# Two-block transformer kernel: in the second layer the gates of the recurrence's branch come first, with their sigmoid, and that branch's products are dealt out in the rounds of heads and softmax

## The reference, cut to what matters

```python
(k_raw, v_raw, i_raw, ff_raw, fb_raw, q_raw, qh_raw, gh_raw,
 four_raw, gate_raw) = jnp.split(h @ w_in[l], IN_SPLITS, axis=-1)
...
o_a = window_attention(q, k, v, kc, vc, attn_sink[l])            # branch 1
o_h, _, _ = hgrn_bidir(hgrn_q(qh_raw), kf, lff, kb, lfb, vh, s_f, s_b)
o_hr = hgrn_readout(o_h, gh_raw, hgrn_norm_g[l])                 # branch 2
o_f = fourier_mix(four_raw)                                      # branch 0
y = merge_branches(o_f, o_a, o_hr, gate_raw, w_branch[l], w_out[l])

def merge_branches(o_four, o_attn, o_hgrn, gate_raw, w_branch, w_out):
    br = jnp.stack([o_four, o_attn, o_hgrn], axis=-2)
    proj = jnp.einsum('btnc,ncd->btnd', br, w_branch)
    gates = jax.nn.sigmoid(gate_raw.reshape(gate_raw.shape[:-1] + (N_BRANCH, D_MODEL)))
    return jnp.sum(gates * proj, axis=-2) @ w_out
```

## Time and profile before

| | before |
|---|---|
| median of 3 runs | 1996.06 us (1993.83 to 1997.84) |
| profiled execution | 1991.99 us |
| its span in the trace | 1990.0 us |
| TensorE busy | 1926.9 us (97%) |
| VectorE, ScalarE, GpSimdE busy | 1235.4, 943.6, 473.7 us |
| second layer: heads / softmax / branches begin | about 1618 / 1695 / 1740 us from the span's start |
| output projection begins | 1775 us |

### The profile page before, as it was taken

The page is one execution under the profiler, slowest core; times in us unless marked ns, Lnnn a source line. Parts: engine busy times, 40 slices in busy tenths (PEclk is TensorE's granted clock), DMA queues, the critical chain, the costliest instruction groups (busy, mean ns, idle before and its releaser), DMA issues.

```text
span 1990.0 us, 30419 instructions
## 1 busy us (share of the span) xinstructions
PE 1926.9 (97%) x12222; PEld 1711.6 (86%) x12222; DVE 1235.4 (62%) x1975; ACT 943.6 (47%) x1502; POOL 473.7 (24%) x322
## 2 busy tenths in 40 slices
PE   8998999899999999999999999999999899899999
PEld 7998888899987888787788888888888898699988
DVE  6877898679856863555663653364376947686410
ACT  5453446555456433426743531233275454765643
POOL 1211022000000000002344254555500000304887
PEclk9999999999999999999999999999999999999999
DMA  8888563467733112211133344466432233154554
GB/s 300 250 276 289 176 220 112 174 212 240 271 129 103 57 43 85 96 53 43 51 109 111 122 160 147 152 220 211 158 108 95 96 128 111 60 170 151 186 193 149
DMA packets 84636, 299.23 MB, mean 150 GB/s; under 512 B 9992, under 2 KB 13200, under 8 KB 84112
## 3 DMA queue, kind: packets, MB, share of 16 engines
q1 hardware_dynamic: 65600, 232.81, 34.2%
q0 software_dynamic: 17280, 60.95, 9.5%
q10 hardware_dynamic: 1616, 3.52, 0.5%
HBM read 296.18 MB, written 4.11 MB: 151 GB/s over the span
## 4 chain that ended last, share of the span: by engine, by line
PE 79%; DVE 10%; ACT 5%; issue 2%; DMA 2%; POOL 1%; DVEq 0%; SPq 0%; ACTq 0%; POOLq 0%
PE ps L586 20%; PE ps L581 20%; PE ps L584 20%; DVE wl L449 3%; PE ps L578 3%; ACT wh L433 2%; PE ps L2036 1%; PE ps L580 1%; PE ps L1236 1%; DMA dilskew<-lines 1%; PE ps L1340 1%; PE ps L1241 1%; PE ps L1238 1%; PE ps L1380 1%; PE ps L1359 1%
## 5 line engine op out<-in xcount | busy, mean ns | idle before, releaser
L581 PE MATMUL ps<-HH,wh 128*128 128x256 f32 (+1 forms) x2160 | 706.4, 327 | 7.8 <-ACT wh L433 3.8
L586 PE MATMUL ps<-HH,wl 128*128 128x256 f32 (+1 forms) x2160 | 693.0, 321 | 11.9 <-DVE wl L449 9.1
L584 PE MATMUL ps<-HL,wh 128*128 128x256 f32 (+1 forms) x2160 | 690.3, 320 | 0.0
L433 ACT ACTIVATE wh<-wr 128x1024 fp32r<-128x1024 f32 x440 | 459.1, 1053 | 345.7 <-PE ps L586 251.0
L449 DVE TENSOR_TENSOR wl<-wr,wh 128x1024 fp32r<-128x1024 f32 x301 | 367.0, 1223 | 191.8 <-ACT wh L433 191.1
L586 PEld LDWEIGHTS ps<-HH,wl 128*128 128x128 f32 x2160 | 412.9, 191 | 45.0 <-DVE wl L449 12.0
L581 PEld LDWEIGHTS ps<-HH,wh 128*128 128x128 f32 x2160 | 413.1, 191 | 43.2 <-issue 9.8
L584 PEld LDWEIGHTS ps<-HL,wh 128*128 128x128 f32 x2160 | 413.2, 191 | 30.8 <-issue 2.4
L449 POOL TENSOR_TENSOR wl<-wr,wh 128x1024 fp32r<-128x1024 f32 x139 | 338.1, 2435 | 220.3 <-ACT wh L433 218.9
L1495 POOL TENSOR_TENSOR s<-s,ST 128x512 f32<-128x512 f32 x56 | 57.4, 1041 | 688.9 <-DVE ST L1463 688.6
L1108 DVE CUSTOM_DVE_ANT_0 PROD<-WM,COND 128x1024 f32<-128x1024 f32 x104 | 127.6, 1240 | 1.3
(11 more groups left out here) (308 smaller groups left out, 3010.7 us busy)
## 6 DMA issues: line engine op xcount, KB each, us to landing
wr<-wstream SPq DMA_DIRECT2D x440, 512.0 KB, 3.3
WM<-wmod POOLq DMA_DIRECT2D x68, 512.0 KB, 4.2
X<-wmod POOLq DMA_DIRECT2D x28, 512.0 KB, 5.3
NAB<-naskew POOLq DMA_DIRECT2D x16, 128.0 KB, 6.0
dilskew<-lines POOLq DMA_DIRECT2D x1, 2048.0 KB, 22.7
DILB<-dilskew POOLq DMA_DIRECT2D x2, 1024.0 KB, 9.3
COND<-cond ACTq DMA_DIRECT2D x2, 1024.0 KB, 4.6
CT<-consts POOLq DMA_DIRECT2D x1, 1216.0 KB, 7.1
```

Source lines behind the costliest of these rows:

```text
L433: ins = e.activation(self.WH[i % NSPL][:, :], self.WR[n % NRAW][:, :], ACT.Copy)
L581: e.matmul(out, wh, xh, start=i == 0, stop=False)
L584: e.matmul(out, wh, xl, start=False, stop=False)
L586: return e.matmul(out, wl, xh, start=False, stop=i == n_k - 1)
```

## The change

In the second layer only (`if l`):

- The gate's tiles come in another order: first the eight of branch 2 (the recurrence's), then branches 0 and 1 for each output tile in turn. `gate_at` and `gate_of` translate; G1 and Y1 are laid out the same way. The first eight are emptied by Sigmoid in place of Copy, and their later sigmoid instructions fall away.
- The products of branch 2 leave the branch stage. They follow the 48 halves of the gate in the same generators as eight more portions of 4 slices (12 products), so there are 56 to deal out. VectorE multiplies a pair of them with its gates into G1 (`dve_gated`); the branch stage adds that to branch 0's product.
- The fill deals out two halves in place of one in rounds 6, 8, 11 and 14 of the heads and in rounds 9 and 10 of softmax. The Fourier halves begin as soon as 48 are done, beside the fill.
- Gate weights are asked for by the half: `make_high` and `make_low` are called at each half, for the blocks up to two past that half's end.

```diff
@@ def pe_gates / act_gates / dve_gates
+    def gate_of(self, l, n):
+        if l:
+            return (n, 2) if n < 8 else ((n - 8) // 2, n % 2)
+        return n // 3, n % 3
+    def gate_at(self, l, d, br):
+        if l:
+            return d if br == 2 else 8 + 2 * d + br
+        return 3 * d + br
...
                 if k == 3:
+                    self.W.step((key, "half"))
                     yield
             self.W.step((key, 0))
             yield
+        if l:
+            for ds in self.turns(l):
+                for _ in self.pe_turn(e, w, l, T, ds, 2):
+                    yield
...
-            self.make_high(e, w, (key, 0))
+            self.make_high(e, w, (key, "half" if l else 0))
             yield
+            if l:
+                self.make_high(e, w, (key, 0))
...
-            ins = e.activation(self.g_ap(l, n), self.main.item(key)[:, 0:T], ACT.Copy)
+            if l and n < 8:
+                self.table(e, "sigmoid")
+            func = ACT.Sigmoid if l and n < 8 else ACT.Copy
+            ins = e.activation(self.g_ap(l, n), self.main.item(key)[:, 0:T], func)
...
+        if l:
+            for d in range(8):
+                self.make_high(e, w, (("branch", l, d, 2), 0))
+                yield
...
+        if l:
+            for ds in self.turns(l):
+                for d in ds:
+                    self.make_low(e, w, "lo_dve", (("branch", l, d, 2), 0))
+                    if d != ds[-1]:
+                        yield
+                self.dve_gated(e, w, l, ds)
+                yield
+    def dve_gated(self, e, w, l, ds):
+        key, gg = ("turn", l, ds, 2), self.g_of(l, ds, 2)
+        for d in ds:
+            w.wait_ge(*self.c("gate").at((l, self.gate_at(l, d, 2))))
+        w.wait_ge(*self.c("dense").at(("branch", l, ds[-1], 2)))
+        e.tensor_tensor(gg, self.of_turn(self.main.item(key), ds), gg, ALU.mult).then_inc(*self.c("br").mark((l, ds, 0)))
+        self.main.release(key, self.c("br"), (l, ds, 0))
@@ def pe_branches / act_branches / dve_branches
-            for br in BRANCHES:
+            for br in self.late_branches(l):
+                for _ in self.pe_turn(e, w, l, T, ds, br):
+                    pass
+    def late_branches(self, l):
+        return BRANCHES[1:] if l else BRANCHES
...
+                if l and turn == 0:
+                    continue
...
+                elif l and turn == 1:
+                    for x in self.tm.before(("acc", l, ds)):
+                        w.wait_ge(*x)
+                    e.tensor_tensor(acc, got, gg, ALU.mult).then_inc(*c.mark((l, ds, 1)))
+                    self.main.release(key, c, (l, ds, 1))
+                    for part in range(2):
+                        w.wait_ge(*c.at((l, ds, part)))
+                    e.tensor_tensor(acc, acc, self.g_of(l, ds, 2), ALU.add).then_inc(*c.mark((l, ds, 2)))
@@ class Fill
     def some(self, turn):
-        for _ in range(min(2 if self.last == 16 and turn < 2 else 1, 44 - self.n)):
+        for _ in range(min(2 if turn in ((0, 1), (6, 8, 11, 14))[self.l] else 1, (44, 56)[self.l] - self.n)):
             self.half()
     def all(self):
-        for _ in range(min(1, 48 - self.n)):
+        self.turn += 1
+        for _ in range(min(2 if self.l and self.turn in (9, 10) else 1, (48, 56)[self.l] - self.n)):
             self.half()
     def gates_or(self, other):
-        if self.n < 48:
-            self.all()
-        else:
+        if self.n >= 48:
             next(other, None)
+        self.all()
```

More of the change, by code:

```diff
@@ L1959, in pe_gates @@
         for n in range(24):
-            c, key = W_IN["gate"] + 1024 * (n % 3) + 128 * (n // 3), ("gate", l, n)
+            d, br = self.gate_of(l, n)
+            c, key = W_IN["gate"] + 1024 * br + 128 * d, ("gate", l, n)
             self.main.take(key)
@@ L1982, in act_gates @@
             yield
+        if l:
+            for d in range(8):
+                self.make_high(e, w, (("branch", l, d, 2), 0))
+                yield
     def dve_gates(self, e, w, l):
         for n in range(24):
-            self.make_low(e, w, "lo_dve", (("gate", l, n), 0))
+            self.make_low(e, w, "lo_dve", (("gate", l, n), "half" if l else 0))
             yield
+            if l:
+                self.make_low(e, w, "lo_dve", (("gate", l, n), 0))
             yield
+        if l:
+            for ds in self.turns(l):
[12 more added lines that the diff above has]
+        self.main.release(key, self.c("br"), (l, ds, 0))
     def o_done(self, l):
@@ L2535, in y_ap @@
     def y_ap(self, l, d, z):
-        return self.Y1[:, 3 * d + z, :] if l else (self.YA, self.YB)[d // 4][:, 3 * (d % 4) + z, :]
+        return self.Y1[:, 8 + 2 * d + z, :] if l else (self.YA, self.YB)[d // 4][:, 3 * (d % 4) + z, :]
     def turns(self, l):
@@ L2543, in g_of @@
     def g_of(self, l, ds, br):
-        n = 3 * ds[0] + br
+        n = self.gate_at(l, ds[0], br)
         if l:
-            return self.G1[:, n:n + 4:3, :]
+            return self.G1[:, n:n + (2 if br == 2 else 3):1 if br == 2 else 2, :]
         return self.GA[:, n:n + 1, :] if n < 12 else self.GB[:, n - 12:n - 11, :]
     def y_of(self, l, ds, z):
-        n = 3 * ds[0] + z
+        n = self.gate_at(l, ds[0], z)
         if l:
-            return self.Y1[:, n:n + 4:3, :]
+            return self.Y1[:, n:n + 3:2, :]
         return self.YA[:, n:n + 1, :] if n < 12 else self.YB[:, n - 12:n - 11, :]
@@ L2571, in pe_branches, with pe_turn @@
             self.tm.take(("acc", l, ds))
-            for br in BRANCHES:
[L2573 to L2580, removed]
+            for br in self.late_branches(l):
[3 more added lines that the diff above has]
+        return BRANCHES[1:] if l else BRANCHES
+    def pe_turn(self, e, w, l, T, ds, br):
+        key = ("turn", l, ds, br)
+        self.main.take(key)
+        for x in self.main.before(key):
+            w.wait_ge(*x)
+        name = ("w_branch_2", l, br, "split" if br == 1 else None)
+        for i, d in enumerate(ds):
+            self.dense(e, w, self.main.item(key)[:, T * i:T * i + T], ("branch", l, d, br), name, range(4),
+                       [(128 * d, 128 * d + 128)], self.branch_rhs(l, br, T))
+            yield
     def act_sigmoids(self, e, w, l, ds, brs):
@@ L2584, in act_sigmoids @@
             for d in ds:
-                w.wait_ge(*self.c("gate").at((l, 3 * d + br)))
+                w.wait_ge(*self.c("gate").at((l, self.gate_at(l, d, br))))
             self.table(e, "sigmoid")
@@ L2595, in act_branches @@
     def act_branches(self, e, w, l, T):
-        turns = self.turns(l)
-        self.act_sigmoids(e, w, l, turns[0], BRANCHES)
+        turns, branches = self.turns(l), self.late_branches(l)
+        self.act_sigmoids(e, w, l, turns[0], branches)
         for n, ds in enumerate(turns):
-            for br in BRANCHES:
+            for br in branches:
                 self.make_high(e, w, *[(("branch", l, d, br), 0) for d in ds])
@@ L3145, in __init__ @@
     def __init__(self, gates, l):
-        self.gates, self.n, self.last = gates, 0, (16, 24)[l]
+        self.gates, self.n, self.last, self.turn, self.l = gates, 0, (16, 24)[l], 0, l
     def half(self):
```

1 line of the change is left out of this document (added).

## The result

| | before | after |
|---|---|---|
| median | 1996.63 us (20 runs, 1993.63 to 2000.92) | 1999.97 us (20 runs, 1996.51 to 2003.40) |
| ratio | | 1.0015, 95% interval 1.0008 to 1.0022 |
| profiled execution | 1991.99 us | 2001.28 us |
| its span | 1990.0 us | 1999.3 us |

A forecast was written before the change was run, and what follows sets the result against it. TensorE, at work for 97% of the span, was taken as the bound, so only its pauses could move. The terms -0.5 + 4.4 - 1.1 - 1.8 + 1.85 gave +2.85 us, median 1998.9, range 1991.8 to 2003.

The forecast's parts named there:

- Rounds 0 to 5: Heads: half-wise weight requests end TensorE's wait for a low half; a gain of 0.5 us, bounds 0 and 0.6.
- Rounds 6 to 8: Heads: gate 16 goes ahead of head 2, whose tile waits 6.1 us for K's bank; a loss of 4.4.
- The lower bound: Heads, rounds 6 to 8: with only K's own chain in between, a pause of 2.7 us and a cost of 1.0.
- Rounds 9 to 14: Heads: round 11's extra half covers the wait before head 3's turn; a gain of 1.1 us, bounds 0 and 1.3.
- Softmax: Softmax stage: extra halves cover waits at the last transposes and values; a gain of 1.8 us, bounds 0.5 and 3.3.
- Branches: Branch stage: VectorE starts later with little to spare, so y is late; 0.35 us at entry, 1.85 in all.
- The sign given: End of the branches: TensorE's first product on y would stand idle 2 us or more.
- Table load: Recurrence: one more sigmoid table load of 1.28 us on ScalarE, covered by its 3.85 us of standing, costs nothing.
- (a): Rival, heads: the bank ring hides the emptying and head 2 waits no longer; -3.25 us, median 1992.8, chance 0.20.
- (b): Rival: all pauses covered, softmax gives its whole 3.3 us, branches lose nothing; -6.6 us, median 1989.5, chance 0.10.
- (c): Rival: VectorE bounds the branches, 2 to 3 us more, median 2001.5, chance 0.25; sign: VectorE has no pause there.
- (d): Rival: the change doesn't do what it says and the halves stay where they were; no chance of its own.

The follow-up runs named there:

- the half requests alone: The kernel before, with only the second layer's gate weights asked for by the half: 1992.15 us, ratio 0.9994.
- the request out of the way: The changed kernel, but gate 16's weight requests come when the gate ends, not at its first half: 1996.97 us, ratio 1.0007.
- the pause filled: The changed kernel with 44 throwaway TensorE products ahead of head 2's tile in the heads: 1997.03 us, ratio 1.0010.
- rounds 8, 11, 13 and 14: The changed kernel with the heads' extra halves in these rounds in place of 6, 8, 11 and 14: 1993.92 us, ratio 0.9996.
- the early cast: ScalarE's cast of the branches' first block put ahead of the last attention copy, added to rounds 8, 11, 13 and 14: 1991.06 us, ratio 0.9977.

## Why the prediction was right or wrong

**The result.** Forecast 1998.9 (+2.85), no change that can be told, leaning to slower: measured 1999.97 and +3.0 us, inside the range (1991.8 to 2003) and the forecast's own (1996.5 to 2001.5). The prediction called 0.2% the bound of what can be told; 20 runs told the 3.0 from zero.

**Rounds 0 to 5, right.** The wait of 0.31 goes (-0.55), and it goes with the half requests alone.

**Rounds 6 to 8, right in mechanism and size, and a term missing.** The mean to the tile is 8.69 us after (1665.94 to 1674.63), worked out as 8.7 (1661.3 to 1670.0); the pauses cost 4.35 for 4.4. Moving the extra half to another round removes it. The lower bound was too low: 2.7 us of pause if only K's own chain stood between. With the request out of the way 4.46 are lost, because head 1's rotation (1.14) still runs ahead of K's scale and can't begin before the turn, for which VectorE was idle 2.03 us. Missing was what a pause of that length does to the work behind it: 2.46 us at the lower clock level, shown by three traces with it (tiles of 5.29, 4.99 and 5.29) and two with the pause filled (2.98 both). The Trainium skill (TensorE: Matmul & The Clock Gate, sections What's actually happening and Wait — 56ns, not 53.3ns?) says that the array's clock is at 1.2 GHz when it has been idle, and gives N / 1.2 GHz as the distance of two products of N columns there; for 256 columns that makes an estimate of 213 ns, and the trace agrees (0.21). I forecast a pause of 6.1 us and priced it as idle time alone.

**Rounds 9 to 14, right in sum.** -1.34 for -1.1. That a pause can come back at another place on the same release is what rounds 8, 11, 13 and 14 showed.

**Softmax, right in sum.** -2.12 for -1.8: the last normalisation starts 0.5 later against the stage's first score (39.11 for 38.62) where 0.7 was assumed, the last transposes idle 0.21 and 0.26 instead of 1.41 and 0.34, some 0.9 lost for the 1.3 predicted, the last values not at all, and one score's wait grew from 0.60 to 0.91, the 0.3 predicted without a row for it.

**Branches, right.** +0.33 and +1.45 for +0.35 and +1.5. VectorE's pair costs 5.53 (two subtractions of the same place in the pair at 1774.85 and 1780.38) for 5.52. The step put the late start down to the last values' buffer; the runs showed a second part in it, the table load and two sigmoids ahead of the cast, and that this one can be had for nothing. The sign given, a first product on y idle 2 us or more, came as 1.69 and then 0.34; what is lost there, 4.93 less 2.4 of work, is the 2.6 of the sum to 0.1.

**Table load, right.** A load (1.28) stands in the recurrence at 1547.18 now, and the recurrence is 92.20 us for 92.21.

**Rivals.** (a) and (b) fell with the 5.81 idle. Rounds 8, 11, 13 and 14 alone give -1.72 in the trace against (a)'s -3.25; with the early cast, which isn't part of (a), it is -3.64. (c) fell, but its sign came: VectorE has no pause over 0.1 us in the branches, from 1764.32 until it waits for the last y at 1786. So the sign was badly chosen, since an engine that is only late from the start doesn't pause either until it has caught up. What tells the two apart is the price of a pair, 5.53 against TensorE's 5.73, and TensorE, which waits nowhere within the pairs behind the 0.61 at the entry. (d) fell too: the extra halves stand in TensorE's rounds.

**What stays open.** In the traces the change costs 4.6 and 4.0, by the times 3.0 and 2.8. One trace of before stands against two of after, the grant dips in places that differ from execution to execution (1.2 and 1.5 us in two traces above), and the intervals reach to 4.4; whether the missing 1.2 to 1.6 us are that, no run separates. That the forecast difference, 2.85, came within 0.2 us of the timed one is therefore in part luck: against the trace the sum was 1.7 too low, by the half clock that it lacked less 0.7 gained elsewhere, and the times happened to show 1.6 less than the trace. A kernel with whole-gate requests and the rest of the change wasn't tried: as I read the program, TensorE would wait for a block for which ScalarE and VectorE wait for TensorE.

## What to carry to other kernels

When work is dealt out into rounds, write down the order in which the ring's banks are taken: one half more in one round put a tile on the one bank whose emptying is slow. Price a long pause of TensorE with the work behind it at half the clock (here 6.05 us became 8.5). And before a stage in which an engine has little to spare, look at what stands in front of its first instruction: here one cast moved into an idle 1.31 us gave 2.0 us, 0.9 near the stage's entry and 1.1 at its far end.

## What the hardware showed unexpectedly

The granted clock followed pauses, but not one to one. Idle 5.81 us: 0.50 in all three traces, for 6.8 us. Idle 4.22: 0.50 as well, for 3.4, in one trace. Idle 1.69 and 0.34 shortly after one another: 0.50 for 3.4 us in one trace, no fall in five others. A pause that cost 6.05 in itself cost 8.5 in all. And the same 3.4 us at 0.50 cost nothing in one place and over a us in another: inside the recurrence they only shortened a wait of TensorE in the trace before (from 1568.5), and made the recurrence 1.22 us longer in the trace of the filled pause (from 1584.2).
